# Forty tiles of the expert table turned by VectorE ahead of the sweep, through DRAM

## The reference

```
q    = RMSNorm(x) @ w_q;  experts, gates = top-16 of the 128 x 128 key sums, softmax
act  = gelu(u[experts] . h) * gates
out  = x + sum over the 128 experts of a token of act * v[expert]
```

## Time and profile before

| what | value |
|---|---|
| time, median of 3 runs (lowest to highest) | 3099.25 us (3099.15 to 3099.84) |
| the profiled execution's own time | 3099.67 us |
| its span | 3097.9 us |
| PE, PEld busy | 2999.4 us (97%), 2674.4 us (86%) |
| DVE, ACT, POOL busy | 2243.1 us (72%), 1012.9 us (33%), 1381.9 us (45%) |
| matmuls of the sweep, three groups of x2048 | 704.5, 687.6, 685.9 us |
| transposes of the sweep (L1819), x2048 | 264.8 us, 272 ns each |
| HBM read, written | 807.61 MB, 53.61 MB |

### The profile page before, as it was taken

One profiled execution on the slowest core, in us unless ns is written; L12 is line 12 of the kernel. 1 busy time (PEld: TensorE's weight loads), 2 busy tenths in 40 slices (PEclk: granted clock), 3 DMA queues, 4 the chain that ended last, 5 costly groups with the idle time before them and its releaser, 6 DMA issues. The chain is left out here.

```text
span 3097.9 us, 41953 instructions
## 1 busy us (share of the span) xinstructions
PE 2999.4 (97%) x15889; PEld 2674.4 (86%) x15889; DVE 2243.1 (72%) x2996; ACT 1012.9 (33%) x1245; POOL 1381.9 (45%) x846
## 2 busy tenths in 40 slices
PE   8999999999889999999999999999999999999998
PEld 6888777788789999999999999999998777787777
DVE  4223655542587787877878787798777889899888
ACT  3112343331323323323323333233323333333333
POOL 1000111100045465555555555566756676666551
PEclk9999999999999999999999999999999999999999
DMA  4333344462368898988889888899999999999996
GB/s 168 101 99 102 109 136 149 149 224 95 99 244 277 310 309 276 335 277 295 308 280 331 276 310 296 296 324 330 323 356 370 413 411 414 414 416 415 415 416 279
DMA packets 296532, 863.29 MB, mean 279 GB/s; under 512 B 59252, under 2 KB 176000, under 8 KB 211904
## 3 DMA queue, kind: packets, MB, share of 16 engines
q0 software_dynamic: 102208, 424.02, 37.5%
q1 hardware_dynamic: 156592, 406.88, 36.2%
q10 hardware_dynamic: 37584, 30.43, 2.9%
HBM read 807.61 MB, written 53.61 MB: 278 GB/s over the span
## 5 line engine op out<-in xcount | busy, mean ns | idle before, releaser
L1572 PE MATMUL ps<-hT_hi,uT_hi 128*128 128x384 f32 x2048 | 704.5, 344 | 9.9 <-DVE uT_lo L1428 9.4
L1574 PE MATMUL ps<-h2T_lo,uT_hi 128*128 128x384 f32 x2048 | 687.6, 336 | 0.0
L1573 PE MATMUL ps<-hT_hi,uT_lo 128*128 128x384 f32 x2048 | 685.9, 335 | 0.0
L678 POOL DMA_INDIRECT gate_grid<-gates,grid_cells x256 | 541.3, 2114 | 127.1 <-issue 80.6
L1428 DVE TENSOR_TENSOR uT_lo<-ps,uT_hi 128x1024 fp32r<-128x1024 f32 x256 | 313.1, 1224 | 215.1 <-ACT uT_hi L963 209.3
L1572 PE MATMUL ps<-v_hi,a_hi 128*128 128x512 f32 x1024 | 407.0, 397 | 40.0 <-DVE v_lo L1478 36.2
L1573 PE MATMUL ps<-v_hi,a_lo 128*128 128x512 f32 x1024 | 403.7, 394 | 0.0
L1574 PE MATMUL ps<-v_lo,a_hi 128*128 128x512 f32 x1024 | 403.6, 394 | 0.0
L1003 ACT ACTIVATE v_hi<-v_raw 128x2048 fp32r<-128x2048 f32 x128 | 245.6, 1919 | 471.6 <-PE ps L1574 321.4
L1572 PEld LDWEIGHTS ps<-hT_hi,uT_hi 128*128 128x128 f32 x2048 | 385.7, 188 | 14.1 <-DVE uT_lo L1428 11.5
L1573 PEld LDWEIGHTS ps<-hT_hi,uT_lo 128*128 128x128 f32 x2048 | 386.0, 188 | 1.9
(11 more groups left out here) (202 smaller groups left out, 4721.6 us busy)
## 6 DMA issues: line engine op xcount, KB each, us to landing
u_tile<-in_peer_u SPq DMA_DIRECT2D x128, 1024.0 KB
v_raw<-in_peer_v SPq DMA_DIRECT2D x128, 1024.0 KB
w_raw<-in_w_in SPq DMA_DIRECT2D x24, 1024.0 KB, 5.0
wc_raw<-in_w_in SPq DMA_DIRECT2D x48, 512.0 KB, 3.7
gate_grid<-zeros POOLq DMA_DIRECT2D x16, 1024.0 KB
products_dense<-products ACTq DMA_DIRECT2D x128, 128.0 KB
dots_at<-products_dense SPq DMA_DIRECT2D x32, 512.0 KB
gates_of<-gate_grid SPq DMA_DIRECT2D x32, 512.0 KB
```

The costliest lines, as they stand in the source:

```text
L678: pool.indirect_dma_start(out=gate_grid, out_offset=bass.IndirectOffsetOnAxis(ap=grid_cells[:, d, col:col + 1], axis=0), in_=gates[:, 2 + ...
L1572: mm(out, a_hi, b_hi, start=first, stop=False)
L1573: mm(out, a_lo, b_hi, start=False, stop=False)
L1574: return mm(out, a_hi, b_lo, start=False, stop=last)
```

## The change

Forty tiles of u, the odd ones among the first 80 (`turned_before`), are turned ahead of time. During projections and heads SyncE loads such a tile whole into `seg_rows` (`load_rows`, rows of 8 KB). VectorE turns it in four instructions (`turn_rows`), each of 128 x 512 in blocks of 32 x 32, into `seg_turned`. SyncE stores it with four DMAs, one per group of 32 partitions, to `uT_all` in DRAM (`keep_turned`), in such an order that a plain load of 128 rows brings the transposed tile back, and then loads the next one. There is one buffer of each, so a turn waits for the load and the stores behind the turn before it. Of the 40 turns one stands ahead of the loop of the projections, three in each of its five rounds, three between it and the heads, and three in each of the first seven heads.

In the sweep SyncE loads odd tiles up to 79 from `uT_all`; ScalarE and VectorE split them from `u_tile[1]` in SBUF and not from PSUM, and TensorE has no transposes for them. Their buffer is free once VectorE has made the second low part (`uT_ready[1]`), where before it was once TensorE had turned it. The loops of SyncE over heads of the sweep are unrolled. ScalarE waits for all 160 stores before its first split of w_out, since `wo0_hi` lies where `seg_rows` did. GpSimd writes zeros once per head in the heads, and the other eight times during the output projection.

```diff
+def turned_before(tile):
+    return tile % 2 == 1 and tile < 2 * TURNED
...
+            def load_rows(n):
+                sp.dma_start(seg_rows[:, :], u_table[bass.ds((2 * n + 1) * P, P), :]).then_inc(seg_in, 16)
+
+            def keep_turned(n, last=False):
+                rows = uT_all[bass.ds(n * P, P), :].rearrange("(r d) (a m) -> a d r m", r=QUADS, a=QUADS)
+                sp.wait_ge(seg_ready, 4 * n + 4)
+                for a in range(QUADS):
+                    sp.dma_start(rows[a], seg_turned[QUAD * a:QUAD * (a + 1), :, :, :].rearrange("d r k e -> d r (k e)"))\
+                        .then_inc(seg_stored, 16)
+                if not last:
+                    load_rows(n + 1)
...
             with sp.Fori(0, CT - 1) as j:
                 for p in range(PIECES):
                     sp.wait_ge(wc_ready, PIECES * j + p + 1)
                     conv_piece(j + (p + 2) // PIECES, (p + 2) % PIECES)
+                    if 1 <= p <= 3:
+                        keep_turned(3 * j + (TURNED_QKV + 1 + p))
...
-                    sp.wait_ge(uT_half1_ps[b % 2], TOPK // 2 * i + b // 2)
-                    sp.dma_start(u_tile[b % 2][:, :], u_table[bass.ds(i * TOPK * P + b * P, P), :])\
-                        .then_inc(u_tile_in[b % 2], 16)
+                    tile, last = TOPK * i + b, TOPK * i + b - 2
+                    if last >= 0 and turned_before(last):
+                        sp.wait_ge(uT_ready[1], last + 1)
+                    elif last >= 0:
+                        sp.wait_ge(uT_half1_ps[b % 2], turned_by_pe(b % 2, last + 1))
+                    source = uT_all[tile // 2 * P:(tile // 2 + 1) * P, :] if turned_before(tile)\
+                        else u_table[tile * P:(tile + 1) * P, :]
+                    sp.dma_start(u_tile[b % 2][:, :], source).then_inc(u_tile_in[b % 2], 16)
...
-                for n in range(2 * j, 2 * j + 2):
-                    pool.dma_start(grid_v[n * P * 8:(n + 1) * P * 8, :].rearrange("(p r) t -> p r t", r=8),
-                                   zeros[:, :].unsqueeze(1).to_broadcast([P, 8, GRID])).then_inc(grid_done, 16)
+                zero_cells(j)
...
+            for n in range(HEADS, ZERO_DMAS):
+                pool.wait_ge(w_ready, 4 * QKV_CHUNKS + n - HEADS + 5)
+                zero_cells(n)
...
+            def turn_rows(n):
+                dve.wait_ge(seg_in, 16 * n + 16)
+                if not (isinstance(n, int) and n == 0):
+                    dve.wait_ge(seg_stored, 16 * QUADS * n)
+                for q in range(4):
+                    v.transpose(seg_turned[:, :, 4 * q:4 * q + 4, :].rearrange("p r k e -> p k r e"),
+                                seg_rows[:, q * CHUNK:(q + 1) * CHUNK].rearrange("p (k r d) -> p k r d", r=QUADS, d=QUAD))\
+                        .then_inc(seg_ready, 1)
...
                 split_wc(j, 3)
+                if not last:
+                    turn_rows(3 * j + (TURNED_QKV + 4))
                 split_wc(j, 4)
...
                     split_wc(j + 1, 1)
+                    turn_rows(3 * j + (TURNED_QKV + 5))
...
                     split_wc(j + 1, 2)
+                    turn_rows(3 * j + (TURNED_QKV + 6))
...
-                        if more:
+                        if more and not turned_before(c + 1):
                             turned(nxt, TOPK // 2 * i + (b + 1) // 2 + 1, half)
+                        elif more and half == 0:
+                            summed.then_inc(uT_half0_ps, 1)
```

More of the change, by code:

```diff
@@ L70 @@
 FIRST_ADDED = 7
+QUAD = 32
+QUADS = P // QUAD
+TURNED = 40
+TURNED_QKV = 3 * (QKV_CHUNKS - 1)
 ZERO_DMAS = 2 * HEADS
@@ L90, with turned_by_pe @@
 WQ_LOADS = (0, 5)
+def turned_before(tile):
+    return tile % 2 == 1 and tile < 2 * TURNED
+def turned_by_pe(parity, end):
+    return sum(tile % 2 == parity and not turned_before(tile) for tile in range(end))
 class Steps:
@@ L229, in late_sb @@
             return nc.alloc_sbuf_tensor_at(name, shape, dt, offset=taken[0] - size)
+        seg_rows = nc.alloc_sbuf_tensor_at("seg_rows", [P, D], F32, offset=late)
+        seg_turned = nc.alloc_sbuf_tensor_at("seg_turned", [P, QUADS, KT, QUAD], F32, offset=late + 8 * KB)
         wo0_hi = nc.alloc_sbuf_tensor_at("wo0_hi", [P, QUARTER, CHUNK], F32R, offset=late)
@@ L297, in decoder_layer @@
         grid_v = gate_grid.rearrange("(e t) o -> e (t o)", t=GRID)
+        uT_all = nc.dram_tensor("uT_all", (TURNED * P, D), F32, kind="Internal").ap()
         mix_all = nc.dram_tensor("mix_all", (KT, P, SEQ), F32, kind="Internal").ap()
@@ L384, in decoder_layer @@
         grid_done = sem("grid_done")
+        seg_in = sem("seg_in")
+        seg_ready = sem("seg_ready")
+        seg_stored = sem("seg_stored")
         u_tile_in = sems("u_tile_in", 2)
@@ L426, in load_quarter, with load_weights @@
                     .then_inc(w_in_raw[q % 2], 16)
-            def load_weights(chunks, weights, before, order=range(4), begun=2):
+            def load_rows(n):
[8 more added lines that the diff above has]
+                    load_rows(n + 1)
+            def load_weights(chunks, weights, before, order=range(4), begun=2, turning=False):
                 def chunk(c, first):
@@ L433, in chunk @@
                         load_quarter(weights, c if q < 2 else c + 1, (q + 2) % 4, order)
+                        if turning and q != (0 if isinstance(c, int) else 1):
+                            keep_turned(3 * c + max(q - 1, 0))
                 chunk(0, begun - 2)
@@ L440, in load_weights @@
                     load_quarter(weights, chunks - 1, q + 2, order)
+                    if turning and q == 0:
+                        keep_turned(TURNED_QKV)
             for t in range(TB):
@@ L448, in _ @@
             load_quarter(w_in_v, 0, 1, range(4))
-            load_weights(QKV_CHUNKS, w_in_v, 0)
+            load_rows(0)
+            load_weights(QKV_CHUNKS, w_in_v, 0, turning=True)
             def conv_piece(j, p):
@@ L460, in _ @@
             conv_piece(0, 1)
+            keep_turned(TURNED_QKV + 1)
             with sp.Fori(0, CT - 1) as j:
@@ L467, in _ @@
                 conv_piece(CT - 1, p + 2)
+                if 1 <= p <= 2:
+                    keep_turned(3 * (CT - 1) + TURNED_QKV + 1 + p, last=p == 2)
             def load_mix(q):
@@ L530, in _ @@
             sp.wait_ge(wq_ready, 4)
-            with sp.Fori(0, PEER_HEADS - 2) as i:
+            sp.wait_ge(seg_stored, 16 * QUADS * TURNED)
+            for i in range(PEER_HEADS - 2):
                 sweep(i, choosing=True)
@@ L547, in _ @@
             load_v(0, 0, 0)
-            with sp.Fori(PEER_HEADS - 2, PEER_HEADS) as i:
+            for i in range(PEER_HEADS - 2, PEER_HEADS):
                 sweep(i, choosing=False)
-            sp.wait_ge(uT_half1_ps[0], TILES // 2)
+            sp.wait_ge(uT_half1_ps[0], turned_by_pe(0, TILES))
             load_v(1, 0, 1)
@@ L557, in _ @@
             load_group(0, 0)
-            sp.wait_ge(uT_half1_ps[1], TILES // 2)
+            sp.wait_ge(uT_half1_ps[1], turned_by_pe(1, TILES))
             load_v(2, 0, 2)
@@ L631, in store_o, with zero_cells @@
                 pool.dma_start(mix_all[j:j + 1].rearrange("k p t -> (k p) t"), o_mix).then_inc(o_stored, 16)
+            def zero_cells(n):
+                pool.dma_start(grid_v[n * P * 8:(n + 1) * P * 8, :].rearrange("(p r) t -> p r t", r=8),
+                               zeros[:, :].unsqueeze(1).to_broadcast([P, 8, GRID])).then_inc(grid_done, 16)
             pool.wait_ge(head_mean, 1)
@@ L745, in split_weights @@
                 if isinstance(c, int) and (c, before) == (0, QKV_CHUNKS) and q < 2:
+                    act.wait_ge(seg_stored, 16 * QUADS * TURNED)
                     nc.scalar.activation((wo0_hi if q == 0 else w_hi[1])[:, :, :], wo_raw0, ACT.Copy).then_inc(w_hi_ready, 1)
@@ L956, in split_u @@
             def split_u(i, b, half):
+                tile = TOPK * i + b
                 if half == 0:
-                    act.wait_ge(uT_half0_ps, TOPK * i + b + 1)
-                else:
-                    act.wait_ge(uT_half1_ps[b % 2], TOPK // 2 * i + b // 2 + 1)
+                    act.wait_ge(uT_half0_ps, tile + 1)
+                if turned_before(tile):
+                    if half == 0:
+                        act.wait_ge(u_tile_in[1], 16 * (tile // 2 + 1))
+                    nc.scalar.activation(uT_hi[half][:, :, :].rearrange("p k (a e) -> p k a e", a=QUADS),
+                                         uT_rows[:, 8 * half:8 * half + 8, :, :], ACT.Copy).then_inc(uT_hi_ready[half], 1)
+                    return
+                if half == 1:
+                    act.wait_ge(uT_half1_ps[b % 2], turned_by_pe(b % 2, tile + 1))
                 nc.scalar.activation(uT_hi[half][:, :, :], ps_uT[half], ACT.Copy).then_inc(uT_hi_ready[half], 1)
@@ L1108, in _ @@
             low(0, 3)
+            def turn_rows(n):
[6 more added lines that the diff above has]
+                        .then_inc(seg_ready, 1)
+            turn_rows(0)
             dve.wait_ge(vec_in, 16 * 10)
```

(12 more changed lines are left out.)

1 line of the change is left out of this document (added).

## The result

The changed kernel takes 3131.7 us, median of 4 runs (3129.89 to 3133.76), beside 3099.2 us for the kernel before (3098.1 to 3099.84). The ratio is 1.0105, 95% interval 1.0088 to 1.0123: slower by 32 us, where 11 us faster was forecast.

A forecast was written before the change was run, and what follows sets the result against it. TensorE, busy 97% of the span, was taken as the bound, though in the heads it waits for ScalarE and VectorE. 3099.67 - 45.5 (sweep) + 34 (heads) = 3088 us, range 3062 to 3114.

The forecast's parts named there:

- Transposes taken from TensorE: Sweep: 1.76 us less per tile, 70.4 in all; after VectorE holds TensorE up, 9.1 per head, -45.5 us.
- The length of a turn: VectorE's four transposes of 128 x 512: 0.62 us each, 2.5 us per turn, ends 1.2 and 4.6.
- Rival 3: Slower: turns at half rate, 4.6 us, or loads 4 us late; heads 7.9 us each, total 3109 us; chance 0.27.
- The projections: Three turns per chunk fit into VectorE's free time: cost 0, at most 5 us if loads come late.
- The heads: Turn in front of the convolution 2.5, later store +1.0, clock and late load +1.4: 4.9 us per head, +34 us.
- Head 0: Priced like the other heads, 4.9 us, with VectorE up to 1 us late behind the `split_wc(j, 3)` turn.
- The clock: Heads: TensorE idle 4 to 5 us restarts at a lower clock, 1.5 us; +1.4 together with VectorE's late load.
- Rival 1: Heads: only the turn's length counts, store lands as before, clock holds; 17.5 us, total 3072 us; chance 0.19.
- Zero writes: Moving eight of GpSimd's zero writes from the heads to behind them changes nothing.

The follow-up runs named there:

- e5: Changed kernel without the turn in front of the convolution: two turns per head, 33 tiles in all; 3067.82 us, 0.9904 of the kernel before.
- e6: Changed kernel with neither turns nor their DMAs in the heads, the sweep still treating 40 tiles as turned; 3057.47 us, 0.9867 of the kernel before.
- e8: e7 with SyncE holding the load behind the turn in front of the convolution until the store of `b_sb` has landed; 3101.32 us.
- e7: Changed kernel without the turn behind `split_wc(j, 3)`, the one in front of the convolution kept, 33 tiles; 3132.41 us, 1.011 of the kernel before.
- e1: Changed kernel with the 21 turns of the heads kept but without their stores and loads; 3081.28 us, 0.9941 of the kernel before.
- e2: Changed kernel with the stores and loads of the heads kept but without their turns; 3103.23 us, 1.0011 of the kernel before.
- e4: Changed kernel with all zero writes in the heads again, two per head; 3132.56 us, 1.011 of the kernel before.

## Why the prediction was wrong, step by step

- **Transposes taken from TensorE: right.** 1.76 us per tile, 70.4 in all, was the right start, and it was right that VectorE would take a third back. In head 2 of the sweep of the changed kernel TensorE waits for VectorE at these places:

```profile
1327.51 0.44 PE L1663 MATMUL ps<-hT_hi,uT_hi 128*128 128x384 f32 x1 [0.23 <-DVE uT_lo L1519]
...
1333.00 0.44 PE L1663 MATMUL ps<-hT_hi,uT_hi 128*128 128x384 f32 x1 [1.03 <-DVE uT_lo L1514]
...
1353.52 0.44 PE L1663 MATMUL ps<-hT_hi,uT_hi 128*128 128x384 f32 x1 [1.81 <-DVE uT_lo L1514]
...
1359.55 0.44 PE L1663 MATMUL ps<-hT_hi,uT_hi 128*128 128x384 f32 x1 [0.71 <-DVE uT_lo L1514]
```

  They are tile 0, tile 1 and both halves of tile 3, 3.8 us, where the same head had a single wait of 0.58 before: 3.2 more, and the forecast was 3.5 more. By the starts of matmuls, tiles 4, 6, 10, 12 and 14 of heads 1 to 4 are each 1.8 us shorter, and tiles 0 to 3 together 0.3 us longer, where the forecast has them even. The 16 tiles of such a head take 177.7 us where they took 186.8, -9.1 as forecast, and heads 5 to 7 are within 1 us of before. The sum over VectorE's own rows, tested against a wait that the old trace had, held.
- **The length of a turn: right**, 2.49 us for four. Rival 3's half rate did not happen: a transpose of 128 x 512 takes 0.67 us. The Trainium skill (VectorE: DVE Perf Modes, The three transpose paths) prices 128 x 128 in bf16 at 311 ns, from which 5.0 us per turn was estimated. Four times that price is 1.24 us, nearly twice what one instruction over 512 float32 columns took here.
- **The projections: cost 0 (at most 5), measured +3.8** (+5.8 and +6.2 in e5 and e6). The load was taken to land 5.0 us after its issue; it takes 7.9, after 3.1 us for the four stores ahead of it. A turn and its round trip are some 14 us where a quarter has 10.75, so VectorE waits up to 9.2 us for a load, in front of a split that TensorE needs. TensorE waits 2.83 us for `wi_lo` at 85.00. Where the other microseconds lie (the first `wc_raw` lands late in e5) no run has taken apart.
- **The heads: here the prediction failed**, at the step "with part of a 5.0 us load in front of it I take +1.0 (0 to 2.4)". The place was right, the chain through `b_sb`, its store, ScalarE and the scores was right, the turn's 2.5 us were right. But the store lands 5.9 us later, not 1.0, outside both ends. The upper end was less than half of a load's 5.0 us; in fact the small store lands no sooner than the whole load, and the load takes 7.9 us and not 5.0. e8 and head 6 show it, e7 shows that the turn behind `split_wc(j, 3)` adds nothing to it in these heads. The forecast had 2.5 + 1.0 + 1.4 = 4.9 us per head. Measured, as a mean of heads 0 to 5: turn 2.5, its own wait for a load 0.7, store 5.9, together 9.1, where the wait in front of the scores grew by 9.0 (from 1.0 to 10.0). The remaining 1.4 of the 10.5 us are of the size that e1 shows for the lower clock.
- **Head 0 was missed as well.** Six distances between heads make 63 us of the 76; 12.8 lie in head 0 (`b_sb` first at 357.2, projections' end at 293.1, before 340.6 and 289.3). The forecast let VectorE be late by up to 1 us behind the turn that follows `split_wc(j, 3)`. In head 0 it waits 4.96 us for that turn's load (at 312.89), nothing hides it, and by e7 that one turn costs 7.8 us. The other 5.0 hold the 2.5 us of the turn in front of the convolution; the rest was not taken apart.
- **The clock: direction right.** From 330 to 590 us the granted clock was 1.00 before and 0.89 now, and after every wait of some 10 us TensorE starts at the lower level. The Trainium skill (TensorE: Matmul & The Clock Gate, HAM oscillation) says that a gap in every turn of a loop brings the clock down in every turn. The changed kernel agrees, in seven heads of seven; e1, with waits of 3.4 us, has six heads of seven, and the 487.20 row of e1 is the one without.
- **Rival 3** was right in direction and in its point of decision (6.5 us per head; it was 10.5), and it named a late load, but as a mishap of the turn's own wait, not as what delays someone else's store. Its 3109 us were still too low, and so was the range's upper end. Rival 1's counterargument, that only what is ahead of the store can delay it, was too narrow: in e2 the load is behind.
- **Zero writes: right**, nothing (e4).

## What to carry to other kernels

Before adding DMA traffic to a stage that looks idle, list the small transfers on whose landing an engine waits there, and keep bulk loads from being issued in the microseconds before them or right behind them: a DMA share of 0.45, as the heads had before, says nothing of such a collision, and one wait on the issuing queue or another place in the program can be worth more than the whole change (e5 and e7 turn the same 33 tiles and differ by 65 us). Price a buffer that is refilled behind its use by its full round trip, issue and landing as they are under the new load, and place uses at least that far apart. An engine's own sum of rows, checked on a wait that the old trace has, predicted well here what happens when it becomes the bound.

## What the runs showed of the hardware

- A store of 256 KB issued by GpSimd beside a load of 1 MB with 8 KB rows from SyncE landed with the load, 8.2 us after its issue, where it takes 2.4 us by itself and 3.6 us behind 1 MB of stores in 2 KB pieces (e8). In the changed kernel's record of single packets its first packet starts 4.1 to 4.3 us after the issue, where that was 1.2 us before and 1.5 in e8; what holds it back is not shown. A load issued 0.3 us behind it delayed it too, to 6.7 us (e2), while 2 MB of zero writes behind it on GpSimd's own queue did not (2.4 us).
- VectorE's STREAM_TRANSPOSE of 128 x 512 float32 in 32 x 32 blocks takes 0.67 us, four in a row 2.49 us, like an elementwise operation of that size (0.68 us), here with a strided output.
- Issuing four stores of 32 partitions took SyncE 2.89 us and a load of 1 MB behind them 0.99 us, when the same load issued by itself took 0.38 us (at 498.92 in e8).
- After waits of 3.4 us TensorE's granted clock fell in six heads of seven (e1), after one of 2.13 us in the kernel before it fell too, and after waits of 1.0 us in none.
